# One buffer for the vector table and its pad, and the modulation products begun four attention units later

## The reference

```python
# attention ("fox") of the first block, 8 heads x 4 query blocks of 128 = 32 units
s = jnp.einsum('bhqd,bhkd->bhqk', qb, kh) * scale + cb[..., None] - c[:, :, None, :]
p = jax.nn.softmax(jnp.where(mask, s, -jnp.inf), axis=-1)
o = jnp.einsum('bhqk,bhkd->bhqd', p, vh)

# modulation of the second block, per layer: 6 * 1024 numbers
mod = jax.nn.silu(c) @ w_ada[l] + b_ada[l]
```

## Time and profile before

| what | value |
|---|---|
| median of three runs | 3017.85 us (3015.26 to 3018.03) |
| the profiled execution | 3016.9 us, its span 3015.1 us |
| PE / DVE / ACT / POOL busy | 93% / 50% / 36% / 30% of the span |
| the stretch of attention | about 422 to 512 us of the span |
| modulation products in attention | 28, one in each of units 0 to 27 |

### The profile page before, as it was taken

How to read it: one execution, slowest core, us unless ns; L and a number is a source line. 1 busy time by engine, 2 the same in 40 slices (tenths; PEclk the granted TensorE clock), 3 DMA queues, 4 the chain that set the end, 5 groups by cost and what they waited for, 6 DMA issues and landing times.

```text
span 3015.1 us, 34366 instructions
## 1 busy us (share of the span) xinstructions
PE 2795.9 (93%) x13302; PEld 2275.9 (75%) x13302; DVE 1519.2 (50%) x1691; ACT 1093.9 (36%) x1229; POOL 894.5 (30%) x196
## 2 busy tenths in 40 slices
PE   7867798899998999999899999889999998999998
PEld 5666565787777888887677888678988877778886
DVE  4633657769973431144237666634311351476666
ACT  3311434367763244233333222233432333332222
POOL 3100110100003234434333444332344343344443
PEclk9789989889999999999999999999999999999999
DMA  4000133659952222222233344322232222334443
GB/s 146 28 0 21 42 111 100 256 201 363 362 196 89 70 70 93 96 86 103 84 119 146 147 181 160 137 70 71 70 105 97 85 92 94 107 147 159 170 158 126
DMA packets 64341, 373.97 MB, mean 124 GB/s; under 512 B 7392, under 2 KB 8416, under 8 KB 28896
## 3 DMA queue, kind: packets, MB, share of 16 engines
q1 hardware_dynamic: 62064, 365.95, 33.7%
q10 hardware_dynamic: 2160, 6.42, 0.6%
HBM read 370.24 MB, written 2.10 MB: 123 GB/s over the span
## 4 chain that ended last, share of the span: by engine, by line
PE 74%; issue 3%; DVE 3%; POOL 1%; ACT 1%; ACTq 0%; DVEq 0%; POOLq 0%
PE pd L239 18%; PE pd L241 18%; PE pd L240 18%; PE pd L255 2%; PE pd L256 2%; PE pd L254 2%; PE pd L1418 2%; PE pd L1420 2%; PE pd L1419 2%; POOL sb_w_lo L217 1%; PE pd L1445 1%; PE pd L1447 1%; PE pd L1446 1%; PE pd L1376 1%; PE px L1571 0%
## 5 line engine op out<-in xcount | busy, mean ns | idle before, releaser
L217 POOL TENSOR_TENSOR sb_w_lo<-sb_raw,sb_w_hi 128x2048 fp32r<-128x2048 f32 x189 | 889.2, 4705 | 2046.5 <-ACT sb_w_hi L208 2046.5
L239 PE MATMUL pd<-sb_h_hi,sb_w_hi 128*128 128x512 f32 x1696 | 678.8, 400 | 44.6 <-DVE sb_h_lo L332 25.6
L240 PE MATMUL pd<-sb_h_lo,sb_w_hi 128*128 128x512 f32 x1696 | 667.8, 394 | 0.0
L241 PE MATMUL pd<-sb_h_hi,sb_w_lo 128*128 128x512 f32 x1696 | 667.3, 393 | 0.0
L208 ACT CAST sb_w_hi<-sb_raw 128x2048 fp32r<-128x2048 f32 x189 | 360.8, 1909 | 331.0 <-PE pd L241 326.9
L239 PEld LDWEIGHTS pd<-sb_h_hi,sb_w_hi 128*128 128x128 f32 x1696 | 322.9, 190 | 124.7 <-DVE sb_h_lo L332 29.7
L239 PE MATMUL pd<-sb_y_hi,sb_w_hi 128*128 128x512 f32 x960 | 382.0, 398 | 27.1 <-issue 17.0
L240 PE MATMUL pd<-sb_y_lo,sb_w_hi 128*128 128x512 f32 x960 | 380.9, 397 | 0.0
L241 PE MATMUL pd<-sb_y_hi,sb_w_lo 128*128 128x512 f32 x960 | 380.9, 397 | 0.0
L240 PEld LDWEIGHTS pd<-sb_h_lo,sb_w_hi 128*128 128x128 f32 x1696 | 323.2, 191 | 69.5 <-issue 2.7
L241 PEld LDWEIGHTS pd<-sb_h_hi,sb_w_lo 128*128 128x128 f32 x1696 | 322.7, 190 | 69.4
(11 more groups left out here) (487 smaller groups left out, 3775.7 us busy)
## 6 DMA issues: line engine op xcount, KB each, us to landing
sb_raw<-in_slabs SPq DMA_DIRECT2D x189, 1024.0 KB, 4.8
sb_V<-in_ada SPq DMA_DIRECT2D x64, 512.0 KB, 6.0
sb_V<-in_moe SPq DMA_DIRECT2D x28, 1024.0 KB, 5.4
sb_QK<-in_moe SPq DMA_DIRECT2D x28, 1024.0 KB, 5.7
sb_raw<-in_moe SPq DMA_DIRECT2D x28, 1024.0 KB, 5.6
sb_ada_early<-in_ada SPq DMA_DIRECT2D x48, 512.0 KB, 4.4
sb_QK<-in_ada SPq DMA_DIRECT2D x32, 512.0 KB, 6.8
sb_xT<-in_x SPq DMA_DIRECT2D x4, 512.0 KB, 5.5
```

What stands on the lines that cost most here:

```text
L217: pool.tensor_tensor(w_lo[j][:], raw[j][:], w_hi[j][:].bitcast(F32), ALU.subtract).then_inc(w_lo_ready[j], 1)
L239: pe.matmul(out, w_hi[j][:, cols], hi[:, k], start=(k == 0), stop=False)
L240: pe.matmul(out, w_hi[j][:, cols], lo[:, k], start=False, stop=False)
L241: last = pe.matmul(out, w_lo[j][:, cols], hi[:, k], start=False, stop=(k == KT - 1))
```

## The change

The two buffers `vec` and `vec_tail` become one buffer of 512 columns, and `mod` is a slice of it. The load of the table writes its first 363 columns. The 28 early products move from DVE's steps 0 to 27 of attention to its steps 4 to 31; the wait for the row `c_row` moves with the first of them. The ring of tiles, the order of the products and their number are the same.

```diff
-        vec = sb("vec", [P, V1_COLS])
-        vec_tail = sb("vec_tail", [P, 512 - V1_COLS])
-        mod = vec_tail[:, 0:ADA_COLS]
+        vec = sb("vec", [P, 512])
+        mod = vec[:, V1_COLS:V1_COLS + ADA_COLS]
...
-            sp.dma_start(vec[:], t["vec1"]).then_inc(vec_loaded, 16)
+            sp.dma_start(vec[:, 0:V1_COLS], t["vec1"]).then_inc(vec_loaded, 16)
...
-                if n < ADA_EARLY:
-                    if n == 0:
+                first = len(UNITS) - ADA_EARLY
+                if first <= n < len(UNITS):
+                    if n == first:
                         dve.wait_ge(c_row_ready, 1)
-                    ada_dot(dve, n, n % ADA_RING, n // ADA_RING, ada_early, c_row, mod[:, n:n + 1])
+                    tile = n - first
+                    ada_dot(dve, tile, tile % ADA_RING, tile // ADA_RING, ada_early, c_row, mod[:, tile:tile + 1])
```

## The result

| kernel | median, us | runs | ratio to before, 95% interval |
|---|---|---|---|
| before | 3016.56 (3009.67 to 3018.03) | 4 | |
| changed | 2990.31 (2988.84 to 2990.94) | 4 | 0.9914 (0.9899 to 0.9930) |
| changed, measured again later | 2989.76 (2984.87 to 2990.87) | 5 | 0.9912 (0.9897 to 0.9926) |

The change made the kernel 0.9% faster, some 26 us; the forecast was 3015.5 and the range ended at 3011.0. The profiled execution has a span of 2989.1 us, 26.0 less than before.

The account below looks back on a forecast made before the run. PE was taken to bound the kernel, holding 74% of the chain. Terms: -3.0 start, -0.4 clock, +0.9 end, 0 buffers = -2.5 us; from the median 3017.85 this gave 3015.35, stated as 3015.5, range 3011.0 to 3020.0.

Parts of the forecast that it names:

- The start: Attention's start: unit 0's scaling, held by POOL's remainder, ends near 429.4 instead of 432.4; PE gains 3.0 us.
- The rival of the copy first: Attention's start: POOL's copy precedes the scaling, gain 2.0, clock low longer; 0.2 us slower to 1.5 faster; chance 0.25.
- the unheld scaling: Rival, attention's start: the remainder does not hold unit 0's scaling; 6.7 us faster, 3011.1; chance 0.05.
- The clock: After PE's idle time at attention's start: a low-clock stretch of 3.4 us again, costing 1.7 instead of 2.1; credit 0.4 us.
- Units 0 to 27 and the end: Attention's remainder: lead carried unchanged, cost 0; at the end the last product delays unit 31's scaling, cost 0.9 us.
- The loads: DMA into the moved buffers: 3% faster by an estimate from the skill; trace disagrees, PE would cover it; nothing credited.
- The buffers: Everything behind `vec` moves 32 bytes; alignment effect on products with moving `y` taken as 0, bounds +20.1 and -16.7 us.
- the 2.5: Whole kernel: the forecast's summed gain in us, from start, clock and end, with buffers at 0.
- alignment helps: Rival, 3348 products with moving `y`: 5 ns each, 16.7 us plus the 2.5, giving 2998.6; chance 0.05.

Follow-up runs that it names:

- the late remainder: Whole change, but POOL copies `c_row` first and makes its remainder after the last scaling: 2986.12 us, ratio 0.9905.
- the 32 bytes: Whole change plus 32 unused bytes between the table and `Y`, so everything behind is 32 bytes off again: 3010.60 us, ratio 0.9988.
- the later remainder alone: One merged buffer, products from unit 0 on as before, POOL's copy ahead of its remainder, which waits for the last scaling: 2986.73 us, ratio 0.9903.

## Why the prediction was wrong

- *The start.* Right. The scaling was held (2.59 us; I had 2.9), DVE went ahead of the copy's work, PE resumed at 428.40, which with the lead of 0.92 is the 429.3 of the old count; I had 429.4. By the rule from the Trainium skill, "SBUF — State Buffer", "Who interferes with whom", that the first to issue gets the shared ports, the scaling goes ahead of the copy. The trace agrees in that order: the scaling was over at 428.35, 0.14 us into the copy. That the copy waited for it the trace does not show, for it took its usual 1.04. The rival of the copy first is refuted, and the unheld scaling too; the late remainder shows what the hold cost.
- *The clock.* Right. After PE's idle time of 2.90 us it fell to 1.2 GHz (0.50) after 428.9, and it rose within 432 to 433, 3.4 us later:

```profile
428.00:429.00 1.00, 0.60 (x2) 0.36 (x3) 0.93 (x3) 0.02 (x1) 1.00 (x2) 0.95 1.02 418
429.00:430.00 1.00, 1.00 (x3) 0.38 (x2) 0.49 (x2) 0.81 (x3) 0.25 (x1) 0.50 1.00 410
...
432.00:433.00 1.00, 1.00 (x6) 0.55 (x5) 0.60 (x1) 0.00 (x0) 0.00 (x0) 0.85 0.00 0
```

- *Units 0 to 27 and the end.* Right term by term. The maximum of unit 3 came 432.40 instead of 436.80, 3.5 us earlier after the lead of 0.92; the terms of the start make 3.4. The last scaling came 0.9 later relative to unit 30's (505.57 - 503.77 against 509.12 - 508.24), as forecast, and 2.6 us are left against 2.5. The last product stands directly ahead of the last reciprocal (505.38):

```profile
503.77 0.42 DVE L1091 TENSOR_SCALAR sb_M<-sb_M,sb_small 128x384 f32<-128x384 f32 x1
504.23 1.23 DVE L348 CUSTOM_DVE_ANT_0 sb_ada_early<-sb_ada_early,sb_T 128x1024 f32<-128x1024 f32 x1
```

Unit 30's scaling before:

```profile
508.24 0.42 DVE L1092 TENSOR_SCALAR sb_M<-sb_M,sb_small 128x384 f32<-128x384 f32 x1
```

- *The loads.* No gain from alignment shows. Those of 1 MB took 6.8 us into `V` in one profile of the changed kernel and 5.4 in another (medians of the whole run), and 5.4 before. The 189 slab loads into `raw` take 4.9 us with `raw` on a multiple of 1024 in the changed kernel and 4.8 in the one with everything 32 bytes off. PE was busy 218.37 of 220 us in the experts (640 to 860 us), 218.66 before.
- *The buffers: "The two contradict each other, so I take 0".* This step failed, and by the starts it is worth 22.8 us of the 26 (20.8 by the medians with and without the 32 bytes, 3010.60 - 2989.76). I compared streamed buffers by their own place and got 395 for the aligned one in the experts and 395 for the unaligned one in a layer. Read with both operands in view, the four rows agree. `y_hi` on `sorted_blk`, both in the region 32 bytes off: 389. `h_lo` on `w_hi`, both aligned: 390. `w_hi` on `sorted_blk` and `y_lo` on `w_hi`, one of each region: 395 and 395. Every slow row crosses the regions, every fast one doesn't. The products that cross are 2880 of `y` on `w`, 288 of `w` on `sorted_blk` and 180 of `y` on `hidT` (which lies over `T`), 3348 in all, by chance the number I had counted otherwise. At 5 to 6 ns they make 17 to 20 us, and with the 2.5 a forecast of 2995 to 2999, near the "alignment helps" rival at 2998.6, to which I gave 0.05. What was left is size: lengths differ by 6 ns, starts by 6.7. One small thing the distance does not explain: `y` on `sorted_blk`, both off alike before, took 229.9 ns from start to start and takes 227.9, some 0.6 us in all.

The Trainium skill, "SBUF — State Buffer", "Who interferes with whom", gives TensorE two independent read ports, one for the streamed operand and one for the held one. The runs do not agree with full independence: a distance of 32 bytes between the two costs 6.7 ns per product of 512 columns. Why, no view shows.

## What to carry over

Two rows that contradict each other under one reading speak against that reading: list for each the place of both operands before pricing the term at zero. Where PE streams one buffer against another for thousands of products, lay both out at the same offset modulo 256 bytes, and compare the group means after any change to the buffers, even one of 32 bytes in a table. And where one engine holds another, move the holder as well: with one buffer, the later remainder alone shortened attention by 5.5 us (85.17 to 79.66), the later products alone by 2.6 (85.17 to 82.56), both by 6.5 (to 78.63).

## What the runs showed that was not expected

- 32 bytes of distance between streamed and held operand cost 6 ns of length (398 against 392) and 6.7 ns from start to start in a product of 512 float32 columns, whichever of the two stands ahead; 256 and 512 cost nothing, 64 slowed two of three groups.
- The opposite for the 256-column value products: with 32 bytes of distance 286 ns against 290, and 118.4 ns from start to start against 121.3. Which sign is needed, and whether other widths do the same, stays open.
- The distances between 128 and 256 bytes were not tried, so a period of 256 is borne out only by its multiples 0, 256 and 512.
